# Taking the next rows' copies ahead of the seventh weight piece in an expert loop

## The reference

```python
def hierarchical_moe(h, wc, bc, wf, bf, w_gate_up, w_down):
    ...
    gates = jnp.sum(jax.nn.one_hot(expert_id, N_EXPERTS, dtype=jnp.float32) * e_w[..., None], axis=1)
    gu = jnp.einsum('nd,edf->nef', xt, w_gate_up)      # 1024 -> 2 x 256 per expert
    gate, up = jnp.split(gu, 2, axis=-1)
    act = jax.nn.silu(gate) * up * gates.astype(h.dtype)[..., None]
    return jnp.einsum('nef,efd->nd', act, w_down).reshape(b, t, d)
```

## Time and profile before

| | us |
|---|---|
| median of 3 runs | 1258.43 |
| lowest, highest | 1256.79, 1260.91 |
| the profiled execution, its time | 1259.16 |
| the profiled execution, its span from first to last instruction | 1257.1 |

### The profile page before, as it was taken

How to read it: one execution, slowest core, us unless ns; L and a number is a source line. 1 busy time by engine, 2 the same in 40 slices (tenths; PEclk the granted TensorE clock), 3 DMA queues, 4 the chain that set the end, 5 groups by cost and what they waited for, 6 DMA issues and landing times.

```text
span 1257.1 us, 19445 instructions
## 1 busy us (share of the span) xinstructions
PE 1141.4 (91%) x7025; PEld 917.7 (73%) x7025; DVE 669.7 (53%) x926; ACT 594.0 (47%) x845; POOL 415.5 (33%) x350
## 2 busy tenths in 40 slices
PE   6998999999999699995799999999989996999990
PEld 4786888778788577884588668886668875788770
DVE  4434324379544899994506122430221336999974
ACT  5545234232424588885233332233332233888871
POOL 4332312110233144435254225442243251334432
PEclk9989999999899899998799999999999997999995
DMA  9232311112126599995443223231222263999945
GB/s 253 66 80 40 69 36 35 51 35 69 51 54 209 213 351 364 373 356 195 157 124 95 62 73 98 87 109 51 76 81 71 68 195 114 342 371 360 379 178 208
DMA packets 89282, 194.86 MB, mean 155 GB/s; under 512 B 19901, under 2 KB 21241, under 8 KB 88186
## 3 DMA queue, kind: packets, MB, share of 16 engines
q1 hardware_dynamic: 67562, 160.00, 38.2%
q10 hardware_dynamic: 11856, 17.07, 4.0%
q0 software_dynamic: 9792, 16.80, 3.6%
HBM read 189.63 MB, written 23.07 MB: 169 GB/s over the span
## 4 chain that ended last, share of the span: by engine, by line
PE 77%; DVE 11%; ACT 4%; DMA 3%; issue 2%; POOL 1%; ACTq 1%; POOLq 0%; SPq 0%; DVEq 0%
PE ps L587 21%; PE ps L589 20%; PE ps L588 20%; PE ps L2252 3%; PE ps L2062 2%; PE ps L2261 2%; PE ps L1917 1%; ACT wh L1152 1%; DVE wl L1733 1%; DMA arena<-y 1%; PE ps L2235 1%; PE ps L1949 1%; DMA arena<-hs,slot_rows 1%; DVE arena L1336 1%; ACTq L1271 1%
## 5 line engine op out<-in xcount | busy, mean ns | idle before, releaser
L749 POOL TENSOR_TENSOR wl<-raw,wh 128x1024 fp32r<-128x1024 f32 x100 | 241.4, 2423 | 488.3 <-ACT wh L915 487.9
L587 PE MATMUL ps<-wh,hT_hi 128*128 128x512 f32 x928 | 376.8, 406 | 16.7 <-DVE hT_lo L1385 8.1
L589 PE MATMUL ps<-wh,hT_lo 128*128 128x512 f32 x928 | 365.0, 393 | 0.0
L588 PE MATMUL ps<-wl,hT_hi 128*128 128x512 f32 x928 | 364.0, 392 | 0.0
L915 ACT ACTIVATE wh<-raw 128x1024 fp32r<-128x1024 f32 x116 | 122.0, 1059 | 246.8 <-PE ps L589 226.5
L587 PEld LDWEIGHTS ps<-wh,hT_hi 128*128 128x128 f32 x928 | 176.0, 190 | 61.3 <-issue 14.2
L589 PEld LDWEIGHTS ps<-wh,hT_lo 128*128 128x128 f32 x928 | 175.6, 189 | 38.5
L588 PEld LDWEIGHTS ps<-wl,hT_hi 128*128 128x128 f32 x928 | 176.2, 190 | 34.5 <-issue 1.0
L587 PE MATMUL ps<-hT_hi,wh 128*128 128x512 f32 x288 | 118.2, 410 | 7.3 <-ACT arena L1063 5.3
L1733 DVE TENSOR_TENSOR wl<-arena,wh 128x1024 fp32r<-128x1024 f32 x96 | 117.0, 1224 | 8.2 <-ACT wh L1152 1.2
L1733 DVE TENSOR_TENSOR wl<-raw,wh 128x1024 fp32r<-128x1024 f32 x92 | 112.3, 1226 | 12.9 <-ACT wh L915 4.6
(11 more groups left out here) (299 smaller groups left out, 1367.9 us busy)
## 6 DMA issues: line engine op xcount, KB each, us to landing
raw<-in_moe_w_gate_up_dram SPq DMA_DIRECT2D x64, 512.0 KB, 9.0
arena<-in_moe_w_gate_up_dram SPq DMA_DIRECT2D x64, 512.0 KB, 9.0
raw<-in_odd_w_in_dram SPq DMA_DIRECT2D x48, 512.0 KB, 3.7
raw<-in_even_w_in_dram SPq DMA_DIRECT2D x32, 512.0 KB, 4.7
arena<-in_moe_w_down_dram SPq DMA_DIRECT2D x32, 512.0 KB, 8.8
raw<-in_moe_w_down_dram SPq DMA_DIRECT2D x32, 512.0 KB, 10.4
arena<-y ACTq DMA_DIRECT2D x8, 1024.0 KB, 8.1
raw<-in_odd_w_out_dram SPq DMA_DIRECT2D x16, 512.0 KB, 3.5
```

Of the source, the lines that this page charges most:

```text
L587: nc.tensor.matmul(dst, lh, rh, start=first, stop=False)
L588: nc.tensor.matmul(dst, lh, rl, start=False, stop=False)
L589: return nc.tensor.matmul(dst, ll, rh, start=False, stop=last)
L749: pool.tensor_tensor(wl[:, i % NSPL, :, :], raw_at(i), wh[:, i % NSPL, :, :].bitcast(F32), ALU.subtract).then_inc(lo_pool, 1)
```

## The change

On ScalarE the two row copies `xT_hi` come before the rounding of piece 7; on VectorE the two row subtractions `xT_lo` come before the low half of piece 7. Nothing is added or left out, and no wait is changed. In the first 14 bodies of each layer the order of the two engines changes; the last two bodies have no row work and stay as they are.

```diff
@@ ScalarE, expert()
                         silu(E + 1, 1 - par, it * 12 + (6 * NE * l + 6 * par + 8))
-                        hi_in(7)
                         if not last:
                             xT_hi(l, it * 2 + (par + 2), par)
+                        hi_in(7)
                     act.wait_ge(s_("ysb_free"), E + 1)
@@ VectorE, expert()
                         gated(E + 1, 1 - par)
+                        if not last:
+                            xT_lo(l, it * 2 + (par + 2), par)
                         lo_in(b + 7, it)
                         if not last:
-                            xT_lo(l, it * 2 + (par + 2), par)
                             lo_in(b + 8, it)
```

## The result

| | us |
|---|---|
| kernel before, median of 6 runs | 1258.74 (1256.79 to 1261.08) |
| changed kernel, median of 6 runs | 1247.01 (1244.25 to 1249.58) |
| ratio, 95% interval | 0.9903 (0.9886 to 0.9921) |
| the same pair, measured a second time | 0.9917 (0.9896 to 0.9937) |

The change makes the kernel 11.7 us faster, 10.4 us in the second measurement (1258.17 to 1247.80). The direction and the releaser were right, and the gain was larger than the sum: the distance that would be left without the stall was put at 0.22 us and is 0.13.

A forecast was written before the change was run, and what follows sets the result against it. TensorE bounds the kernel, stalled in the expert loops by late row subtractions. 7.9 + 1.3 + 0.3 = 9.5 us, less 0.5 for DMA, is 9.0; forecast 1250 us, 8 in 10 for 1247 to 1255.

The forecast's parts named there:

- The releaser: Expert loop: L587, the first gate-up matmul, waits for row subtractions hT_lo, starting 0.22 to 0.26 us after their end.
- the sum: Gain in the expert loops: 7.9 + 1.3 (body 1) + 0.3 (body 14), together 9.5 us before DMA takes some back.
- The size of the unstalled distance: Expert loop, aT transposes to L587: 0.55 us in most bodies would become 0.22, priced from eight transposes taking 0.81.
- rival 1: Issue floor 0.31 to 0.40 us at L587, or VectorE not below 9.6 a body; gain 4.5 to 6.9 us; chance 0.18.
- ScalarE's part: Row copies start 0.81 us after the first xT transpose, piece 7 at +1.77; delays hidden in idle gaps, cost nothing.
- VectorE: Row subtractions end at +2.84 us instead of +3.99, before TensorE wants them at +3.67, so the stall goes.
- Piece 7's margin: Low half ends at +4.1 us, second gate-up piece at +5.37: 1.0 us left after release, the next to be late.
- DMA: Loads fall further behind in shorter bodies: 0.5 us taken back, between 0 and 1, late in layer 1; layer 0 free.
- The hard form of rival 2: Loads are not there sooner, so the expert loops keep 9.79 us a body; gain 1.3 + 0.3, 1257.6 us; chance 0.04.

The follow-up runs named there:

- act_only: Against the kernel before, only ScalarE's row copies moved ahead of piece 7's rounding, VectorE's order unchanged: 1291.82 us in one run.
- rows_last: Against the kernel before, VectorE takes the row subtractions behind the low half of piece 8: 1364.70 us in one run.
- aT_twice: Against the changed kernel, the two aT transposes issued twice, four in all, same result: 1253.67 us in one run.
- aT_4x: Against the changed kernel, eight aT transposes issued in place of two, same result: 1268.87 us in one run.
- dve_only: Against the kernel before, only VectorE's row subtractions moved ahead of piece 7's low half, ScalarE as before: 1249.07 us, ratio 0.9916.
- pad_1us: Against the changed kernel, one extra ScalarE copy (0.95 us) ahead of piece 7's rounding in the looped bodies: 1247.52 us in one run.
- pad_2us: Against the changed kernel, two extra ScalarE copies (1.9 us) ahead of piece 7's rounding in the looped bodies: 1268.00 us in one run.
- half_after: Against the changed kernel, the second half of each weight piece of the middle experts isn't loaded: 1246.69 us, ratio 0.9915.

## Why the prediction was nearly right, and which step failed

**The releaser: right.** The stall was put down to `hT_lo`, not to the rounding that the wait column names. The row subtractions moved earlier took it away, moved later (act_only, rows_last) made it longer, by 1.14 us where 1.3 were worked out and by 2.50 where 2.5 were, and the 0.23 us between their end and `L587` stayed.

**The size of the unstalled distance: the step that failed.** The prediction took 0.22 us from `aT` to `L587`, the upper end of the 0.20 to 0.22 from two eighths of the 0.81 us of eight transposes. It is 0.13. The price per piece of a long row was carried over to a short one, and the two transposes that were to be priced are cheaper than that (aT_twice, aT_4x); why isn't shown. With 0.13 the sum is 24 x 0.42 + (0.77 + 0.68) + 2 x 0.25 = 12.0 us instead of 9.5. Measured by bodies: 0.41 in each of 24 is 9.8 of it. This term is 2.5 us too small, and rival 1 (a floor of 0.31 to 0.40, from body 0) looked for the error on the wrong side. Body 0 has 0.30 after the change too; its TensorE is held up before the transposes.

**ScalarE's part: right, and unneeded.** The copies start 0.64 us behind the first transpose, not 0.81; piece 7 starts at +1.62, not +1.77. It costs nothing, as said, but brings nothing either: dve_only has the same time.

**VectorE: right.** The subtractions end at +2.69 (+2.84 forecast). VectorE doesn't become the bound: it waits for ScalarE within bodies of 9.38 us.

**Piece 7's margin: right, but it isn't the next to be late.** 1.0 us was forecast, and pad_1us and pad_2us enclose it. By the prediction's own figures piece 3 is nearer: ready at +7.3 for +8.1, 0.8 us apart before any release is taken off, against 1.27 for piece 7. In the changed kernel it is 0.94 us (511.57 to 512.51) against 1.34 (508.43 to 509.77), and in pad_1us piece 3 is the one that delays TensorE.

**DMA: right kind, too small.** 0.5 us were taken back, all in layer 1, with layer 0 free by 1.2 us. In the profiles late loads cost 1.2 and 0.3 us in the two layers, then 0 and 0.9, and in dve_only nothing. The body is shorter than was reckoned (9.38 for 9.46), which adds 0.08 a body to how far loads fall behind, 0.9 over 11 bodies; that and the run decide. In layer 0 the late loads came with the short body 0 (9.56 us) and not with the long ones (11.16), which gave the loads 1.6 us more; in layer 1 there is no such order. half_after shows that it is the loads. The limit of about 358 GB/s that the Trainium skill ("DMA: Bandwidth & Descriptors", "Where 436 GB/s comes from") states weighed in the prediction: the loop ran at 366 GB/s over 94 us and at 388 in body 0, above it, and the measurement decides. The hard form of rival 2 did not come about: the bodies got shorter though the DMA engines were 0.99 busy. At 3.55 MB a body of 9.38 us would want 378 GB/s, an estimate; the pieces loaded ahead covered the rest almost to the loops' ends.

**The rest.** 12.0 less 1.5 for late loads is 10.5, where the loops of the first pair gave 10.4. In the second pair body 1 had no extra stall, so the sum is 11.4, less 0.9 again 10.5, and the loops gave 10.2. The medians of the two measurements give a gain of 11.7 and 10.4, with intervals of 9.9 to 14.4 and 7.9 to 13.1 that both hold 10.5; the difference between the two measurements can't be told from noise. With 0.13 in place of 0.22 the forecast would have been 1250 less 2.5, up to 1 us more for DMA, so 1247.5 to 1248.5, and a range as wide as the one given, set around it, would have held both results.

## What to carry to other kernels

When a wait on several semaphores is blamed on one instruction, line up the starts over many repetitions: the true releaser keeps a constant distance. Price the unstalled case from the same instruction count, not from a share of a longer row. And when a reordering spans two engines, ask what each half does alone: here one half gave all the gain, and the other half alone cost three times as much.

## What the hardware showed that was not expected

A wait of 2.7 us in each body brought TensorE to its lower clock (1.2 GHz) behind the wait in every body: granted clock 0.50 in the first 2.4 us behind it, 0.87 over the body, 1.4 us lost a body (rows_last). A wait of 1.3 us in each body did not (act_only, granted clock 1.00 over a body, 10.93 us, which is the 9.79 + 1.14 that the longer wait explains).

The same idle time of 1.84 us stands before body 0 of both layers in all thirteen profiles. Behind it the granted clock of the next 5 us was 1.00 ten times and 0.66 sixteen times, whatever the kernel, and body 0 took about 9.6 us or, in the kernels with two transposes, about 11.1.

Behind two transposes between dense matmuls the next matmul started after 0.13 us, behind four after 0.36, behind eight after 0.79; in a body's length the two and six that were added cost 0.15 and 0.63 us.
